# Decode attention: keys turned in 32x32 blocks on VectorE, block-diagonal queries, sets of one sequence

## What is computed

```python
def stick_breaking_weights(z, mask):
    log_keep = jnp.where(mask, jax.nn.log_sigmoid(-z), 0.0)
    remain = lax.cumsum(log_keep, axis=z.ndim - 1, reverse=True)
    return jnp.exp(jnp.where(mask, z + remain, -jnp.inf))

def sb_decode(q, k_new, v_new, k_past, v_past, bias):
    z_past = jnp.einsum('bqhd,bkhd->bhqk', q, k_past)
    z_new = jnp.einsum('bqhd,bkhd->bhqk', q, k_new)
    z = jnp.concatenate([z_past, z_new], axis=-1) * scale + bias
    a = stick_breaking_weights(z, mask)
    return (jnp.einsum('bhqk,bkhd->bqhd', a[..., :P], v_past)
            + jnp.einsum('bhqk,bkhd->bqhd', a[..., P:], v_new))
```

## Time and profile before

| | us |
|---|---|
| median of 3 runs | 1451.14 |
| lowest, highest | 1446.97, 1455.94 |
| span of the profiled execution | 1442.7 |
| PE busy | 1288.7 (89%) |
| DVE busy | 400.6 (28%) |
| ACT busy | 353.6 (25%) |

### The profile page before, as it was taken

How to read it: one execution, slowest core, us unless ns; L and a number is a source line. 1 busy time by engine, 2 the same in 40 slices (tenths; PEclk the granted TensorE clock), 3 DMA queues, 4 the chain that set the end, 5 groups by cost and what they waited for, 6 DMA issues and landing times.

```text
span 1442.7 us, 22498 instructions
## 1 busy us (share of the span) xinstructions
PE 1288.7 (89%) x8892; PEld 778.3 (54%) x8892; DVE 400.6 (28%) x745; ACT 353.6 (25%) x575; POOL 87.3 (6%) x146
## 2 busy tenths in 40 slices
PE   7999999989999999878999999789987888788782
PEld 4787555756777666546888865533332333333231
DVE  2012565634544445431101123511111001101103
ACT  2122344444554445642000011200000000000000
POOL 3000000020000002000000000011101000100000
PEclk9999999999999989999999999889999889999887
DMA  6113301068999989999911150299999999999985
GB/s 237 59 59 117 111 1 61 27 182 302 386 375 381 379 303 386 385 386 348 392 35 37 59 235 31 88 367 427 424 425 426 425 426 426 426 425 426 427 367 198
DMA packets 119641, 395.96 MB, mean 274 GB/s; under 512 B 17075, under 2 KB 25284, under 8 KB 107250
## 3 DMA queue, kind: packets, MB, share of 16 engines
q1 hardware_dynamic: 109506, 380.41, 67.7%
q0 software_dynamic: 5984, 11.18, 2.2%
q10 hardware_dynamic: 4048, 2.93, 0.6%
HBM read 386.06 MB, written 16.27 MB: 279 GB/s over the span
## 4 chain that ended last, share of the span: by engine, by line
PE 79%; issue 7%; SPq 7%; DMA 4%; DVE 2%; ACT 1%; POOLq 0%; DVEq 0%
PE ps L1180 17%; PE ps L1002 8%; PE ps L694 8%; PE ps L1203 7%; PE ps L824 5%; PE ps L697 5%; PE ps L1005 4%; PE ps L1067 4%; SPq L411 3%; PE ps L858 3%; SPq L399 3%; PE ps L835 3%; DMA arena<-in_w_in 2%; DMA arena<-in_cache_k 1%; PE ps L1191 1%
## 5 line engine op out<-in xcount | busy, mean ns | idle before, releaser
L1180 PE MATMUL ps<-arena 128*64 128x512 f32 x512 | 253.8, 654 | 69.3 <-issue 67.8
L1181 PE MATMUL ps<-arena 128*64 128x512 f32 x512 | 254.3, 655 | 0.0
L1180 PEld LDWEIGHTS ps<-arena 128*64 128x64 f32 x512 | 74.2, 151 | 215.0 <-issue 212.9
L824 PE MATMUL ps<-ident,arena 128*128 128x128 f32 x1024 | 142.8, 283 | 25.4 <-DMA arena<-in_cache_k 24.9
L824 PEld LDWEIGHTS ps<-ident,arena 128*128 128x128 f32 x1024 | 112.3, 143 | 91.3 <-issue 59.3
L1410 ACT ACTIVATE arena<-ps 128x512 f32<-128x512 f32 x192 | 108.2, 596 | 162.7 <-PE ps L824 162.5
L1002 PE MATMUL ps<-mixers,arena 128*128 128x272 f32 x512 | 121.6, 399 | 4.9 <-DMA arena<-in_w_in 4.9
L694 PE MATMUL ps<-mixers,arena 128*128 128x272 f32 x512 | 119.3, 393 | 0.0
L1002 PEld LDWEIGHTS ps<-mixers,arena 128*128 128x128 f32 x512 | 98.8, 194 | 25.9 <-DMA arena<-in_w_in 5.1
L694 PEld LDWEIGHTS ps<-mixers,arena 128*128 128x128 f32 x512 | 96.7, 190 | 20.3 <-issue 0.4
L1821 DVE COPY arena<-ps 128x512 f32<-128x512 f32 x64 | 44.2, 691 | 163.9 <-PE ps L824 163.9
(11 more groups left out here) (343 smaller groups left out, 1393.2 us busy)
## 6 DMA issues: line engine op xcount, KB each, us to landing
arena<-in_cache_k SPq DMA_DIRECT2D x256, 256.0 KB, 5.6
arena<-in_w_gate_exp SPq DMA_DIRECT2D x32, 2048.0 KB, 32.4
arena<-in_w_up_exp SPq DMA_DIRECT2D x32, 2048.0 KB, 36.9
arena<-in_cache_v SPq DMA_DIRECT2D x252, 256.0 KB, 5.9
arena<-in_w_down_exp SPq DMA_DIRECT2D x22, 2048.0 KB, 37.6
mixers<-in_w_down_exp SPq DMA_DIRECT2D x10, 2048.0 KB, 37.7
arena<-in_w_in SPq DMA_DIRECT2D x7, 2048.0 KB, 9.4
arena<-in_w_in SPq DMA_DIRECT2D x8, 1024.0 KB, 15.6
```

What stands on the lines that cost most here:

```text
L824: last = turn(ps[:, turned_at(n, j), P * c:P * c + P], keys_of(n)[:, j, P * c:P * c + P], ident[:, :])
L1180: mm(ps[0:BLK, 1 + u, :], own, wgv[w][:, k, :], start=k == 0, stop=k == KD - 1)
L1181: last = mm(ps[BLK:P, 1 + u, :], own, wuv[w][:, k, :], start=k == 0, stop=k == KD - 1)
```

## The change

A set is now four units of one sequence, 16 pages in order of time. Keys are not turned by PE: DVE turns each unit in two instructions of 128x1024, which transpose 32x32 blocks within their 32 partitions (`keys_turned`, L1859). A partition quarter g then holds features of keys 32g to 32g+31 of each page. The queries are laid out to match (`wq`): for each block of 32 features the queries of one sequence stand once in each quarter, block-diagonally, 8 columns for each quarter. `unit_scores` (L856) becomes 16 products of 128 columns, and a score row belongs to a pair of heads, a quarter, a head and a query. The running sum in a row so covers only its own quarter's keys, 32 of each page; two small products on PE (`other_losses`, L866 and L867) add what the other three quarters lose later, and DVE subtracts that one unit later (`remains`, L1885). `set_weights` writes its result in another order, so that after the turn of the weights key k of page j stands on partition 4k+j; each page of values is loaded onto every fourth partition, four rows of 2 KB to a partition, and `unit_values` (L890) takes 8 columns of weights for each quarter. The queries are copied by 16 extra products and a DVE copy at the last head of the prompt's attention, and every eight units DVE lays out the next sequence's. POOL rebuilds two masks for `other_losses`.

```diff
-            def turn_pages(n, pair):
-                pe.wait_ge(S(f"cache_k_{n % 3}"), (n // 3 + 1) * 16 * GP)
...
-                    for c in range(CT):
-                        last = turn(ps[:, turned_at(n, j), P * c:P * c + P], keys_of(n)[:, j, P * c:P * c + P], ident[:, :])
...
             def unit_scores(n):
...
-                pe.wait_ge(S("kT_act"), 3 * n + 3)
-                pe.wait_ge(S("kT_dve"), n + 1)
+                pe.wait_ge(S("keys_turned"), 2 * n + 2)
+                if n % SEQ_UNITS == 0:
+                    pe.wait_ge(S("q_blocks"), max(n // SEQ_UNITS, 1))
                 if s == 0 and m:
                     pe.wait_ge(S("set_softplus"), 4 * m - 3)
-                for c in range(CT):
-                    last = mm(ps[32 * c:32 * c + 32, ZB, :], qblk_of(m // NGRP, s, c), d_kt[:, n % 2, c, :],
-                              start=s == 0, stop=s == PER_SET - 1)
+                for x in range(4):
+                    for c in range(CT):
+                        last = mm(ps[32 * c:32 * c + 32, ZB, P * s:P * s + P], wq[:, m // SETS_OF % 2, 4 * c + x, :],
+                                  d_kt[:, n % 2, 4 * c + x, :], start=x == 0, stop=x == 3)
                 last.then_inc(S("unit_scores"), 1)
+
+            def other_losses(m):
+
+                pe.wait_ge(S("set_ends"), m + 1)
+                if m == 0:
+                    pe.wait_ge(S("quarters"), 1)
+                own, bank = d_ends[:, m % 2], others_at(m)
+                mm(ps[:, bank, 0:16], neg_lt, own[:, 0:16], start=True, stop=False)
+                mm(ps[:, bank, 0:16], tri_ge, own[:, 1:17], start=False, stop=True).then_inc(S("other_losses"), 1)
...
-                turn_pages(n, (0, 1))
-                if n:
-                    unit_scores(n - 1)
-                else:
+                if n == 0:
                     attn_values(CT - 1)
-                turn_pages(n, (2, 3))
+                unit_scores(n)
...
+                if s == 1 and m:
+                    other_losses(m - 1)
                 if s == 2 and m:
                     turn_weights(m - 1)
...
-                    sp.wait_ge(S("page_turned"), GP * (n - 2))
+                    sp.wait_ge(S("keys_turned"), 2 * (n - 2))
...
-                    sp.dma_start(values_of(n)[:, j, :], a["cache_v"][0, bass.ds(page, 1)].rearrange("a s h d -> (a s) (h d)")
-                                 ).then_inc(S(values_signal(n)[0]), 16)
+                    sp.dma_start(values_of(n)[j::GP], a["cache_v"][0, bass.ds(page, 1)].rearrange(
+                        "a (g s) h d -> (a s) g (h d)", g=4)).then_inc(S(values_signal(n)[0]), 16)
...
+            def keys_turned(n):
+                dve.wait_ge(S(f"cache_k_{n % 3}"), (n // 3 + 1) * 16 * GP)
+                if n >= 2:
+                    dve.wait_ge(S("unit_scores"), n - 1)
+                for half in range(2):
+                    out = d_kt[:, n % 2, :, 64 * half:64 * half + 64].rearrange("p b (j k) -> p j b k", j=2)
+                    v.transpose(out, keys_of(n)[:, 2 * half:2 * half + 2, :].rearrange("p j (b k) -> p j b k", k=32)
+                                ).then_inc(S("keys_turned"), 1)
...
+            def remains(m):
+                chain.wait()
+                dve.wait_ge(S("other_losses"), m + 1)
+                v.tensor_tensor(each(d_z, 16), each(d_z, 16), ps[:, others_at(m), 0:16].unsqueeze(2).to_broadcast([P, 16, 32]),
+                                ALU.subtract).then_inc(S("set_sums"), 1)
...
-                keys_out(n)
+                keys_turned(n)
+                if n % SEQ_UNITS == 2 and 2 <= n // SEQ_UNITS + 1 < NB:
+                    query_blocks(n // SEQ_UNITS + 1)
...
                 if m and s == 0:
                     losses(m - 1)
+                if m and s == 1:
+                    remains(m - 1)
```

More of the change, by code:

```diff
@@ L1823, in losses @@
             def losses(m):
+                own = d_ends[:, m % 2]
                 dve.wait_ge(S("set_softplus"), 4 * m + 3)
                 rounding(d_e, d_t)
+                if m >= 2:
+                    dve.wait_ge(S("other_losses"), m - 1)
+                if m:
+                    dve.wait_ge(S("set_ends"), m)
+                before = d_ends[:, (m - 1) % 2, 0:1] if m % SETS_OF else d_c[:, 1 + m // SETS_OF:2 + m // SETS_OF]
+                chain(v.tensor_copy(own[:, 16:17], before))
@@ L1835, in losses @@
-                dve.wait_ge(S("set_sums"), 2 * m + 1)
-                v.tensor_tensor(d_z, d_z, d_R, ALU.subtract).then_inc(S("set_sums"), 1)
+                chain(v.tensor_tensor_scan(out=d_R[:, ::-1], data0=d_t[:, ::-1], data1=d_ln[:, ::-1],
+                                           initial=own[:, 16:17], op0=ALU.add, op1=ALU.add))
+                chain.wait()
+                v.tensor_copy(own[:, 0:16], each(d_R, 16)[:, :, 0]).then_inc(S("set_ends"), 1)
+                chain(v.tensor_tensor(d_z, d_z, d_R, ALU.subtract))
@@ L1876, in _ @@
                     hgrn(k)
-            losses(NSET * NGRP - 1)
+            losses(SETS - 1)
+            remains(SETS - 1)
             values_out(1)
```

181 lines of the change are left out of this document (99 added, 82 removed).

## The result

The changed kernel takes 1516.4 us (median of 4 runs, 1512.5 to 1520.6); before, beside it, 1449.1 (1443.8 to 1456.0). The ratio is 1.0462, with a 95% interval of 1.0422 to 1.0503: slower, some 67 us, where 35 were forecast. The profiled execution spans 1517.0 us for the 1442.7 of before, 74 us more. The 8 us that the text ahead puts around the span of before are thus mostly something else: the execution profiled there was 6 to 7 us faster than the median.

The account below looks back on a forecast made before the run. DVE was to bound the decode loop through its waits: 20 us of layout, 14 of clock falls and 1 ahead of the loop sum to +35, 1451 + 35 = 1486 us; range 1430 to 1530, the forecast case's own 1466 to 1530.

Parts of the forecast that it names:

- DVE bound through its waits: Decode loop: DVE becomes the bound by a little, 5.87 us a unit against the DMA's 5.45; forecast case chance 0.46.
- the middle price: DVE's transposes of 128x1024: 1.22 us each, 2.45 a unit, with 1.4 and 4.7 a unit kept as ends.
- The group of 46.95 us: Eight units laid out on DVE, 38 us work and 9 waits, against 44.7 before; four groups to unit 36 give +9.
- the clock: PE falls to 1.2 GHz after idling at eleven places up to unit 52: 20 us at most, 14 taken.
- +11: Units 36 to 52, laid out the same way: 105.5 us for the 94.2 of before.
- -6 + 6: Units 52 to 54 cost +6 (two ACT waits, one wide product); the DMA, further ahead from unit 54, gives back 6.
- I take no change: DMA term: value pages keep their 128 runs of 2 KB, so the new loads were priced at no change.
- the draw: Rival: DVE at 5.5 to 5.8 us a unit with few clock falls, 1437 to 1466 us; chance 0.22.
- the fast rival: Rival: DMA the only bound, DVE needing at most 5.45 us a unit, 17 us less, 1434; chance 0.18.
- Ahead of the loop: Before the decode loop: 16 PE products (1 us) and some DVE operations lying in DVE's wait for PE, +1 us.
- Dear transposes: Rival: DVE transposes at 2.35 us each, 144 us more, about 1610; chance 0.14 shared with slow loads.
- Slow value loads: Rival: value pages on 32 partitions load at 231 GB/s, +115 us, 1550 to 1600; chance 0.14 shared with dear transposes.

Follow-up runs that it names:

- the filled kernel: The changed kernel with 16 products of the identity with itself behind TensorE's other work of each unit from unit 4: ratio 1.0853 to before.
- their run: The changed kernel with SyncE issuing the keys of units 5 and 6 ahead of its wait for the new rows: 1510.8 us, ratio 1.0420.
- single edits: The changed kernel with only keys turned one unit ahead (1499.2 us), or only plain value loads (1509.6 us, computation not right).
- both edits: The changed kernel with keys turned one unit ahead and plain value loads together (computation not right): 1455.2 us, ratio 1.0018.

## Why the prediction was right, and where its sizes were off

**DVE bound through its waits: right.** The transposes took 1.217 us for 1.22 laid out. The rule of the Trainium skill that the prediction cited (Vector Engine (DVE) Microarchitecture Reference, the reshape front-end and per-opcode configuration: one element per cycle and lane) made the middle price the right one, and the trace agrees: 1217 ns for 1024 elements, 1.19 ns an element against the slope of 1.05 of the two-operand operation in the earlier trace rows. The waits stood where the layout had them: `remains` waited 2.5 us on the mean (14.8 over six; laid out 1.7), the first piece 2.6 (2.3). Turning one unit ahead, with nothing else changed, removes the waits for PE. Behind the late keys of the start, nearly all waits were for PE or ACT up to unit 52, as forecast. With plain value loads, so with this bound alone, the kernel takes 1.0390 of before: the direction and the bound were no luck. That 67 us fell inside the range and not only 35 is owed to a range that reached to 1530.

**The group of 46.95 us measured 51.5: the waits were mis-sized.** Laid out were 8.7 us of waits and 38.2 of all else; measured are 15.1 in the four rows above and 36.3 of all else. The layout used full-clock durations for PE. TensorE ahead of pieces 1 and 3, units 20 to 28:

```profile
448.37 1.93 PE L856 MATMUL ps<-arena 128*32 128x128 f32 x32 [6.59 <-DVE arena L1859]
450.24 1.12 PE L876 MATMUL ps<-ident,arena 128*128 128x128 f32 x4
...
472.80 1.94 PE L856 MATMUL ps<-arena 128*32 128x128 f32 x32 [4.58 <-DVE arena L1859]
474.66 1.12 PE L876 MATMUL ps<-ident,arena 128*128 128x128 f32 x4
475.71 1.90 PE L890 MATMUL ps<-arena 128*8 128x128 f32 x32
477.54 1.65 PE L966 MATMUL ps<-arena 128*64 128x128 f32 x8
```

After an idle stretch of 6.59 or 4.58 us the products run at 1.2 GHz (1.93 for the 1.08 of the filled kernel's row above, 1.90 for 1.06, 1.65 for 1.09, and the turn 1.12 for the 0.5 laid out): 1.5 us ahead of piece 1 and 2.9 ahead of piece 3, 4.4 together. DVE waited 3.5 and 4.3 us there in place of the 1.8 and 0.9 laid out, 5.1 more. In the other two groups the clock was down in a third place that the layout did not have, ahead of the second `remains`:

```profile
414.19 1.94 PE L856 MATMUL ps<-arena 128*32 128x128 f32 x32
```

```profile
417.20 0.69 DVE L1885 TENSOR_TENSOR arena<-arena,ps 128x512 f32<-128x512 f32 x1 [3.48 <-PE ps L867]
```

`remains` waits 3.5 and 3.8 us there, and 2.1 us in the group of units 20 to 28, which is the shortest (50.6). The term "the clock", 14 us for eleven places, thus fell due in full and more: 4.4 us a group are 18 up to unit 36 already, an estimate from the group shown, and in the long pieces PE stayed at half clock (0.57 from 540 to 618 us). This is read from rows; no run isolates it.

**The sum, term by term.** Units 12 to 36: +20.3 measured from the pieces (154.4 for 134.0) for 3 x 2.25 and the clock's part. Units 36 to 52: +25 for +11 and the clock's part. Units 4 to 12: +13.6, first product to first product, for +2.25; behind it stand the late keys of the start, worth 6 us by their run, which is not clear of noise; in its trace unit 12 comes 4.7 us earlier. From unit 52 to the gate product: +4.4 where -6 + 6 was forecast. With the +3.4 ahead of unit 4 that makes the 66.7 us at the gate product.

**The value loads, "I take no change": a term put at nothing that was not.** I compared landing and run count and took SyncE's queue as free because it never ended a wait in the kernel before. The landing was right (4.3 us for values, 4.2 for keys), the issue was not looked at: 0.74 us a DMA instead of 0.47. It made a second limit at 51.0 us a group, of which 5.9 x 8 = 47 us are unbroken issuing; why some issues take up to 1.5 us longer (in the kernel before too, one of 3.17 us at 477), which makes up the rest, stays open. In the changed kernel as it stands it costs only 10 us; but it takes away what the DMA was forecast to give back: with plain loads unit 52 to the gate product is 67.7 us, with strided ones 72.7. The DMA share of 1.05 forecast behind unit 52 did not come: 0.89 at 305 GB/s from 660 to 715. With it priced, the draw and the fast rival would have been out: relieved of its waits for PE, the loop still ran at 51.0.

**"Ahead of the loop", +1: too low.** The first product of unit 4's piece comes 3.4 us later. The first VectorE waits (3.8 and 3.9 us for new rows) now stand between transposes, and SyncE's wait for the new rows is 7 us later than before (320.5 us for 313.4), so the keys of unit 5 were late by 5.8 us.

**The rivals.** A DMA-bound loop exists, at 44.5 us a group and 385 GB/s, once both limits are removed, and it ties with the kernel before instead of beating it by 17 us: the loop before was already that fast in units 12 to 36 (134.0 us for 134.8); against its trace this kernel is 13.5 us behind at unit 12 and makes up 6.7 between unit 36 and the gate product. Dear transposes: no (and their 144 us give 1595 on the kernel before or 1630 on the forecast, not "about 1610"). Slow value loads: not with every fourth partition.

## What to carry to other kernels

When a change recuts a transfer, price its issue on the queue that issues it as well as its landing: SyncE's list is an engine with a bound of its own. A span compared with a median hides how fast the profiled execution was: compare spans with their own run. Two limits of the same height hide each other, and single edits (20 and 10 us) then say little about what both are worth (64 us). Where an in-order list holds both waiting work and the work that feeds the bound, put the feeding work one step ahead: here it cost one moved call.

## What the runs showed of the hardware that was not expected

- A DMA of 256 KB in 128 runs of 2 KB takes SyncE 0.47 us to issue as 128 partitions x 1 run and 0.74 us as 32 partitions x 4 runs. ScalarE takes about as long for the second (2.91 us for four), and operations behind the issues in its list wait: one 6.31 us behind eight of them.
- Landing on every fourth partition runs at full speed (383 GB/s from 440 to 480 us with ScalarE issuing, 385 with plain loads); on 32 neighbouring ones the whole stream falls to 223 GB/s at a share of 1.06.
- ScalarE's exponential with a permuted output (four-element steps over 512) takes 1121 ns; the same operation in order took 630 ns.
- With PE at a granted clock of 0.85 the loop with both edits still ran at the DMA's 385 GB/s, 44.5 us for eight units.
- After 6.59 and 4.58 us without work PE's next products ran at 1.2 GHz (1.93 us for 1.08), after 2.20 and 1.52 us at 2.4 GHz; ahead of 414 us they fell to 1.2 GHz with no idle time just before.
